# Two gate tiles between the steps of an attention, and mask and maximum in one operation

## The chip, the cores and the metric

The kernel runs on one core of a Trainium2 chip. The metric is the device time of one execution in microseconds. TensorE (PE in the rows) multiplies matrices into PSUM, VectorE (DVE) and ScalarE (ACT) work element by element, GpSimd (POOL) does one kind of subtraction here, and SyncE (SP) issues the loads. Each engine runs its own instructions in their order and waits for the others by semaphores.

## What is computed

Two transformer blocks on 512 tokens of 1024 features, in fp32. The first has four mixers with residuals between them: windowed attention with a sink beside a retention, a memory cross-attention, a gated convolution, and a second memory cross-attention. The second block adds three gated branches (pooling, latent attention, memory attention) and a mixture of 32 experts. The change touches three attentions:

```python
# windowed attention with a sink (8 query heads of 64 features)
scores = jnp.where(valid, einsum(q, k) * d ** -0.5, NEG_INF)
m = jnp.maximum(jnp.max(scores, axis=-1), sink_logit)
p = jnp.exp(scores - m)
denom = jnp.sum(p, axis=-1) + jnp.exp(sink_logit - m)
# latent attention (8 heads), causal
s = jnp.where(k_idx <= q_idx, s * scale, NEG_INF_2);  p = softmax(s)
# memory attention of the second block (4 heads of 128, 256 memory rows), and its gate
y_mem = softmax(q @ k.T * 128 ** -0.5) @ v
merged = gates[:, 0] * (y_pool @ w_br_pool) + gates[:, 1] * (y_mla @ w_br_mla) \
         + gates[:, 2] * (y_mem @ w_br_mem)     # gates = sigmoid(h @ w_gate + b)
```

## The kernel before

Activations lie with features in the 128 partitions and tokens in the columns. A weight matrix is a stream of *units*, 128x1024 blocks, that pass through a ring of three slots: SyncE loads a unit into `w_ring`, ScalarE rounds it into `hi_ring` (`highs_through`, called by `unit_done`), and GpSimd takes the rest into `lo_ring` (`lows`). A slot is loaded again when its low part is done, and rounded again when TensorE has used it. Each product is three products of rounded parts (`three`). `tile` makes one 128x512 output from one unit with 24 of them; `piece` makes a part of a tile, so that a tile can be spread between the steps of something else. Output tiles go round the four PSUM banks `G`; `bank_free` waits until the tile four before has been evacuated.

An attention runs in units `u` (a query tile of 128 tokens, for one or two heads), of which four are in flight: `S` holds the scores of two, two banks of `G` those of the others. For each, TensorE makes scores, VectorE the maximum (`maxima`, into `mx`, and its scaled negative in `nb`), ScalarE the exponentials and their sum (`exps`), VectorE the normalisation (`normalise`), TensorE the transposes (`transposed`), ScalarE the copy out of PSUM (`copy_t`), and TensorE the value products.

In the windowed attention (`swa_max`, 16 units, two heads each, 128 or 256 keys) VectorE first adds the mask to the scores of each head, then reduces, compares with the sink, negates, and makes `snk`, the sink less the maximum. TensorE puts a quarter of a gate tile (`e_ag`, `e_bg`) into each step. In the latent attention (`top`, 32 units, one head each, 128 to 512 keys) the mask covers the last 128 keys. In the second block's memory attention (`scores2`, `one2`, `top2`; 8 units, 4 value products `x2_o`) TensorE has nothing between the steps. Behind it `branch("g_mem", ...)` runs: for every two output tiles two gate tiles from `xa_hi`, and two products with the memory attention's output `yb_hi`, `yb_lo`. The order on all engines is the order in which the program is written. TensorE's product helper is line 1617 and its transposes in the attentions line 1723, so all their rows have these lines.

## Time and profile before

| | us |
|---|---|
| median of three runs | 1772.3 |
| lowest and highest run | 1771.83, 1773.69 |
| the profiled execution | 1771.13 |
| its span | 1769.3 |
| TensorE busy | 1683.5 (95%) |
| VectorE busy | 872.1 (49%) |
| ScalarE busy | 579.2 (33%) |
| GpSimd busy | 541.7 (31%) |

All times in rows count from the start of the span. Products are pipelined: a product's row lasts longer than the distance to the next one, so distances between starts are what adds up. The granted clock is the share of TensorE's full speed of 2.4 GHz; 0.5 is its other level, 1.2 GHz.

### The profile page before, as it was taken

Reading aid. Unit: us, or ns where it says so; the run is one execution under the profiler, and the core shown is the slowest. Engines: PE = TensorE matmul, PEld = TensorE weight load, DVE = VectorE, ACT = ScalarE, POOL = GpSimd, SP = SyncE. Lnnn points to the kernel's source line nnn. Section 1 sums busy time; section 2 is a strip of 40 time slices with the busy share of each in tenths; the row PEclk is TensorE's granted clock in tenths of the full one; section 3 lists DMA queues with packets and bytes.
Section 4 is the critical chain, followed back from the end, with each engine's and each line's share of the span. In section 5 each row is a group of like instructions: output and inputs, shape, how many; then the busy total and the mean of one; then the engine's idle time right before and its main releaser. Section 6 shows DMA issues by size and latency. Waiting matters only on the chain.

```text
span 1769.3 us, 20751 instructions
## 1 busy us (share of the span) xinstructions
PE 1683.5 (95%) x7816; PEld 1260.4 (71%) x7816; DVE 872.1 (49%) x1420; ACT 579.2 (33%) x952; POOL 541.7 (31%) x228
## 2 busy tenths in 40 slices
PE   6999889999999999999998999999989979999996
PEld 4887658887888888887875768888767755556553
DVE  4338576125644466435666754342323554343335
ACT  4116554324322244334424233342333331121112
POOL 3431216731444446732431214464324300000000
PEclk8999999999999999999999999999989989999998
DMA  4221213521232223421220113243213449888871
GB/s 161 95 72 48 72 48 115 172 96 58 92 95 96 95 84 123 163 83 40 93 84 24 60 49 95 96 131 107 84 36 99 165 183 364 323 344 336 340 287 49
DMA packets 50627, 228.08 MB, mean 129 GB/s; under 512 B 6000, under 2 KB 6896, under 8 KB 45936
## 3 DMA queue, kind: packets, MB, share of 16 engines
q1 hardware_dynamic: 48816, 222.08, 35.8%
q10 hardware_dynamic: 1728, 4.87, 0.8%
q8 instruction: 56, 0.92, 0.2%
q14 instruction: 27, 0.22, 0.0%
HBM read 224.82 MB, written 2.10 MB: 128 GB/s over the span
## 4 chain that ended last, share of the span: by engine, by line
PE 90%; DVE 6%; ACT 2%; issue 1%; DMA 0%; ACTq 0%; DVEq 0%; SPq 0%
PE G L1617 72%; PE O L1617 6%; PE S L1617 5%; PE TR L1617 4%; PE TR L1723 1%; DVE mx L973 1%; DVE mx L978 1%; PE G L2156 0%; DVE arena L993 0%; DVE sq L993 0%; ACT arena L545 0%; DVE S L971 0%; DVE U L1608 0%; DVE yb_lo L1004 0%; DMA X<-in_x_in_dram 0%
## 5 line engine op out<-in xcount | busy, mean ns | idle before, releaser
L484 POOL TENSOR_TENSOR lo_ring<-w_ring,hi_ring 128x1024 fp32r<-128x1024 f32 x222 | 541.3, 2439 | 880.8 <-ACT hi_ring L503 880.5
L503 ACT ACTIVATE hi_ring<-w_ring 128x1024 fp32r<-128x1024 f32 x222 | 234.7, 1059 | 687.9 <-PE G L1617 685.7
L1617 PE MATMUL G<-xa_hi,hi_ring 128*128 128x512 f32 x928 | 378.9, 408 | 19.7 <-POOL lo_ring L484 12.3
L1617 PE MATMUL G<-xa_hi,lo_ring 128*128 128x512 f32 x928 | 369.1, 398 | 0.0
L1617 PE MATMUL G<-xa_lo,hi_ring 128*128 128x512 f32 x928 | 369.0, 398 | 0.0
L1617 PEld LDWEIGHTS G<-xa_hi,hi_ring 128*128 128x128 f32 x928 | 176.5, 190 | 64.2 <-issue 14.1
L1617 PEld LDWEIGHTS G<-xa_lo,hi_ring 128*128 128x128 f32 x928 | 176.6, 190 | 42.1 <-issue 1.9
L1617 PEld LDWEIGHTS G<-xa_hi,lo_ring 128*128 128x128 f32 x928 | 176.1, 190 | 42.1
L1617 PE MATMUL G<-yb_hi,hi_ring 128*128 128x512 f32 x388 | 154.1, 397 | 0.0
L1617 PE MATMUL G<-yb_hi,lo_ring 128*128 128x512 f32 x388 | 151.9, 391 | 0.0
L1617 PE MATMUL G<-yb_lo,hi_ring 128*128 128x512 f32 x388 | 151.8, 391 | 0.0
L932 DVE TENSOR_TENSOR arena<-G,RB 128x512 f32<-128x512 f32 x76 | 52.4, 691 | 192.3 <-PE G L1617 191.5
L1617 PEld LDWEIGHTS G<-yb_hi,hi_ring 128*128 128x128 f32 x388 | 73.3, 189 | 16.3 <-issue 1.0
L1617 PEld LDWEIGHTS G<-yb_lo,hi_ring 128*128 128x128 f32 x388 | 73.3, 189 | 16.2 <-issue 1.0
L1617 PEld LDWEIGHTS G<-yb_hi,lo_ring 128*128 128x128 f32 x388 | 73.2, 189 | 15.4
L901 DVE TENSOR_TENSOR sumsq<-sumsq,sq 128x512 f32<-128x512 f32 (+1 forms) x59 | 74.5, 1263 | 2.7 <-ACT sq L516 2.7
L1617 PE MATMUL G<-cm_hi,hi_ring 128*128 128x256 f32 (+1 forms) x224 | 72.1, 322 | 0.0
L1617 PE MATMUL G<-cm_hi,lo_ring 128*128 128x256 f32 (+1 forms) x224 | 70.7, 315 | 0.0
L1617 PE MATMUL G<-cm_lo,hi_ring 128*128 128x256 f32 (+1 forms) x224 | 70.6, 315 | 0.0
L1617 PE MATMUL O<-arena 128*128 128x128 f32 (+2 forms) x224 | 59.8, 404 | 9.3 <-ACT arena L545 5.6
L1532 DVE TENSOR_TENSOR X<-X,S 128x512 f32<-128x512 f32 x64 | 44.0, 688 | 38.5 <-PE S L1617 38.5
L1617 PE MATMUL G<-yb_hi,xa_hi 128*128 128x256 f32 x256 | 60.2, 294 | 2.9 <-DVE yb_hi L1491 2.9
(300 smaller groups left out, 2674.3 us busy)
## 6 DMA issues: line engine op xcount, KB each, us to landing
w_ring<-in_stream_dram SPq DMA_DIRECT2D x222, 512.0 KB, 3.4
arena<-in_w_gu_dram SPq DMA_DIRECT2D x16, 2048.0 KB, 8.1
ex_rings<-in_w_dn_dram SPq DMA_DIRECT2D x40, 512.0 KB, 13.2
ex_low<-in_w_gu_dram SPq DMA_DIRECT2D x8, 2048.0 KB, 12.4
ex_rings<-in_w_gu_dram SPq DMA_DIRECT2D x8, 2048.0 KB, 12.5
arena<-in_w_dn_dram SPq DMA_DIRECT2D x16, 512.0 KB, 11.6
sq<-in_w_dn_dram SPq DMA_DIRECT2D x8, 512.0 KB, 15.1
X<-in_x_in_dram SPq DMA_DIRECT2D x8, 256.0 KB, 5.7
```

Of the source, the lines that this page charges most:

```text
L484: nc.gpsimd.tensor_tensor(lo_ring[:, s, :], w_ring[:, s, :], hi_ring[:, s, :], ALU.subtract).then_inc(low, 1)
L503: nc.scalar.activation(hi_ring[:, m % RING, :], w_ring[:, m % RING, :], ACT.Copy).then_inc(high, 1)
L901: nc.vector.tensor_tensor(sumsq[:, 0:w], sumsq[:, 0:w], sq[:, (base + f) % 2, 0:w], ALU.add).then_inc(ssq, 1)
L932: nc.vector.tensor_tensor(dst, G[:, a % BANKS, 0:w], by, ALU.mult).then_inc(evac, 1)
L973: do(nc.vector.tensor_reduce(mx[:, at(u), 0:heads], s, AX.X, ALU.max))
L978: do(nc.vector.scalar_tensor_tensor(mx[:, at(u), 0:heads], mx[:, at(u), 0:heads], scale, sink, ALU.mult, ALU.max))
L1532: nc.vector.tensor_tensor(X[:, f, :], X[:, f, :], S[:, f % 2, :], ALU.add).then_inc(x_add, 1)
L1617: return nc.tensor.matmul(*args, **kw)
L1723: ins = nc.tensor.transpose(TR[:, b * P:(b + 1) * P], prob(probs, u, b * P, (b + 1) * P), ident[:, :])
```

## The change

Windowed attention: a new `negative_maxima` does, for each head, one operation that adds the mask, multiplies by the negative scale, writes the result over the scores and keeps the minimum of it and of the negated sink, which is `nb`. `snk` is one subtraction from it. The exponential then has scale -1. A vector `nsink` with the negated sinks is made once at the start. Latent attention: `maxima` reduces the columns ahead of the mask, and one operation masks the last 128 and carries the maximum on. Memory attention of the second block: the first two tiles of `g_mem` are cut into eight pieces, one behind the scores of each step; its scores move from banks 2 and 3 to banks 1 and 2, since the first gate tile uses bank 3 and the second bank 0; ScalarE rounds the next weight unit ahead of its last copy.

```diff
+        nsink = sb("nsink", [P, KT])
...
         def score(u, lo, hi):
-            first = ACC0["e_ag"] + u // TT if u < SU["x0"] else 0
+            first = ACC0["e_ag"] + u // TT if u < SU["x0"] else 3 if u >= SU["x2"] else 0
...
-                                             bias=nb[:, at(u), h:h + 1], scale=scale,
+                                             bias=nb[:, at(u), h:h + 1], scale=-1.0 if sink else scale,
...
                 if u + 3 < 8:
                     one2(u + 3)
+                if u == 6:
+                    unit_done("g_mem", 0)
...
+                if mask is None:
+                    do(nc.vector.tensor_reduce(mx[:, at(u), 0:heads], s, AX.X, ALU.max))
                 else:
+                    low = NEG
+                    if mask_at:
+                        do(nc.vector.tensor_reduce(mx[:, at(u), 1:2], score(u, 0, mask_at), AX.X, ALU.max))
+                        low = mx[:, at(u), 1:2]
+                    part = score(u, mask_at, width)
+                    do(nc.vector.tensor_tensor_reduce(part, part, mask, 1.0, low, ALU.add, ALU.max,
+                                                      mx[:, at(u), 0:1]))
...
+            def negative_maxima(u, width, scale, mask, sink):
+                dve.wait_ge(s_full, u + 1)
+                for h in range(2):
+                    part = score(u, h * width, (h + 1) * width)
+                    note(nc.vector.tensor_tensor_reduce(part, part, mask, -scale, nsink[:, sink + h:sink + h + 1],
+                                                        ALU.add, ALU.min, nb[:, at(u), h:h + 1]))
+                settle()
+                nc.vector.tensor_tensor(snk[:, at(u), 0:2], nb[:, at(u), 0:2], nsink[:, sink:sink + 2],
+                                        ALU.subtract).then_inc(s_max, 1)
...
+            sinks = vec[:, VECTORS["sink"][0]:VECTORS["sink"][0] + KT]
+            do(nc.vector.tensor_scalar(nsink[:, :], sinks, -1.0, None, ALU.mult))
...
-            def branch(stage, k0, ready):
+            def branch(stage, k0, ready, begun=0):
                 for f in range(0, KT, 2):
                     a = ACC0[stage] + 2 * f
                     for e in range(2):
-                        tile(stage, f // 2 * 3 + e, xa_hi, xa_lo, acc=a + e)
+                        if f + e >= begun:
+                            tile(stage, f // 2 * 3 + e, xa_hi, xa_lo, acc=a + e)
...
             def scores2(u):
                 hp, t = divmod(u, TT)
-                if u in (0, 2):
-                    pe.wait_ge(evac, ACC0["xq"] + (2 if u == 0 else 4))
+                if u in (0, 2, 3):
+                    pe.wait_ge(evac, ACC0["xq"] + (2, 2, 3, 4)[u])
...
+                e, ks = ((0, (0, 1)), (0, (2, 3)), (0, (4, 5)), (0, (6,)), (0, (7,)), (1, (0, 1, 2)), (1, (3, 4, 5)),
+                         (1, (6, 7)))[u]
+                if u == 5:
+                    pe.wait_ge(o_free, 24 + 2)
+                piece("g_mem", e, xa_hi, xa_lo, ks)
                 if t == TT - 1:
                     pe.wait_ge(pt_ready, base + u + 1)
...
-            pe.wait_ge(o_free, 24 + 2)
-            branch("g_mem", 0, lambda kk: (o_free, 24 + kk + 1))
+            branch("g_mem", 0, lambda kk: (o_free, 24 + kk + 1), begun=2)
```

TensorE, in the second block's memory attention from the first transposes on, before (TR the transposes, S and G from `arena` the scores):

```order
L1723 MATMUL TR<-ident,arena 128x128 [waits prob_t_ready,score_norm]
L1723 MATMUL TR<-ident,arena 128x128 x3
L1617 MATMUL S<-arena 128x256 [waits score_exp]
L1617 MATMUL S<-arena 128x256
L1723 MATMUL TR<-ident,arena 128x128 [waits prob_t_ready,score_norm]
```

And now, G from `xa_hi` and `xa_lo` the gate tile:

```order
L1733 MATMUL TR<-ident,arena 128x128 [waits prob_t_ready,score_norm]
L1733 MATMUL TR<-ident,arena 128x128 x3
L1627 MATMUL S<-arena 128x256 [waits score_exp]
L1627 MATMUL S<-arena 128x256
L1627 MATMUL G<-xa_hi,hi_ring 128x512 [waits acc_evacuated,unit_low]
L1627 MATMUL G<-xa_lo,hi_ring 128x512
L1627 MATMUL G<-xa_hi,lo_ring 128x512
L1627 MATMUL G<-xa_hi,hi_ring 128x512
L1627 MATMUL G<-xa_lo,hi_ring 128x512
L1627 MATMUL G<-xa_hi,lo_ring 128x512
L1733 MATMUL TR<-ident,arena 128x128 [waits prob_t_ready,score_norm]
```

Six products of the first gate tile now stand between the scores and the next transposes.

VectorE, one step of the windowed attention with 256 keys, before:

```order
L971 TENSOR_TENSOR S<-S,RBm 128x256 [waits score_full,dve_order]
L971 TENSOR_TENSOR S<-S,RBm 128x256
L973 TENSOR_REDUCE mx<-S 128x2 [waits dve_order]
L978 SCALAR_TENSOR_TENSOR mx<-mx,vec 128x2 [waits dve_order]
L980 TENSOR_SCALAR nb<-mx 128x2 [waits dve_order]
L981 TENSOR_TENSOR snk<-vec,mx 128x2
```

And now:

```order
L988 ISA S,nb<-S,RBm,nsink 128x256 [waits score_full]
L988 ISA nb 128x1
L988 ISA S,nb<-S,RBm,nsink 128x256
L988 ISA nb 128x1
L991 TENSOR_TENSOR snk<-nb,nsink 128x2 [waits dve_order]
```

Each fused operation is followed by an instruction that writes out its accumulator; the reduction and two small operations are gone, and three waits of VectorE for itself have become one.

## Rows read from the trace of the kernel before

**Rows 1.** The page: the chain that ended last, by engine; rounding of units.

```profile
PE 90%; DVE 6%; ACT 2%; issue 1%; DMA 0%; ACTq 0%; DVEq 0%; SPq 0%
...
L503 ACT ACTIVATE hi_ring<-w_ring 128x1024 fp32r<-128x1024 f32 x222 | 234.7, 1059 | 687.9 <-PE G L1617 685.7
```

**Rows 2.** Busy time by stretch: length, each engine (instructions), granted clock, DMA.

```profile
143.10:200.20 57.10, 52.65 (x313) 44.09 (x313) 48.54 (x148) 38.17 (x102) 9.43 (x4) 1.00 0.15 52
1269.00:1300.40 31.40, 23.56 (x83) 14.77 (x81) 16.36 (x44) 16.30 (x45) 2.34 (x1) 0.78 0.09 30
```

**Rows 3.** TensorE's timeline, windowed attention: start, duration, instruction [idle before it].

```profile
149.45 0.60 PE L1723 MATMUL TR<-ident,sq 128*128 128x128 f32 x4
...
150.57 0.59 PE L1617 MATMUL G<-xa_hi,hi_ring 128*128 128x512 f32 x1
150.99 0.39 PE L1617 MATMUL G<-xa_lo,hi_ring 128*128 128x512 f32 x1
...
153.11 0.60 PE L1723 MATMUL TR<-ident,sq 128*128 128x128 f32 x4
...
157.10 1.16 PE L1617 MATMUL O<-arena 128*128 128x128 f32 x8 [1.15 <-ACT arena L545]
158.10 0.38 PE L1723 MATMUL TR<-ident,arena 128*128 128x128 f32 x2
```

**Rows 4.** Waits, windowed attention: who waited for whom, us, times, longest.

```profile
ACT arena L532 <- DVE snk L981: 10.1, 6, 2.3
...
PE O L1617 <- ACT arena L545: 4.2, 6, 1.2
```

**Rows 5.** VectorE's timeline, windowed attention; then the mask additions' min/median/max.

```profile
148.31 2.06 DVE L978 SCALAR_TENSOR_TENSOR mx<-mx,vec 128x2 f32<-128x2 f32 x1
...
151.54 0.76 DVE L971 TENSOR_TENSOR S<-S,RBm 128x256 f32<-128x256 f32 x2
152.33 0.69 DVE L973 TENSOR_REDUCE mx<-S 128x2 f32<-128x512 f32 x1
...
153.33 0.15 DVE L981 TENSOR_TENSOR snk<-vec,mx 128x2 f32<-128x2 f32 x1
153.45 0.16 DVE L988 TENSOR_TENSOR den<-den,esnk 128x2 f32<-128x2 f32 x1
...
L971 DVE TENSOR_TENSOR G<-G,RBm x16: 422/424/433, 140.2 to 189.5; 128x256 f32<-128x256 f32 x16
L971 DVE TENSOR_TENSOR S<-S,arena x16: 289/294/300, 932.6 to 1028.4; 128x128 f32<-128x128 f32 x16
```

**Rows 6.** TensorE's timeline, memory attention of the second block and gate tiles.

```profile
1275.20 1.11 PE L1723 MATMUL TR<-ident,arena 128*128 128x128 f32 x4 [2.51 <-DVE arena L993]
...
1277.81 0.88 PE L1723 MATMUL TR<-ident,arena 128*128 128x128 f32 x4
...
1282.62 1.97 PE L1617 MATMUL O<-arena 128*128 128x512 f32 x4
1284.43 1.88 PE L1617 MATMUL G<-arena 128*128 128x512 f32 x4
1288.44 0.99 PE L1723 MATMUL TR<-ident,arena 128*128 128x128 f32 x4 [2.13 <-DVE arena L993]
...
1300.40 0.79 PE L1617 MATMUL G<-xa_hi,hi_ring 128*128 128x512 f32 x1
...
1311.94 0.40 PE L1617 MATMUL G<-yb_hi,hi_ring 128*128 128x512 f32 x1
```

**Rows 7.** Busy time by microsecond, columns as in rows 2.

```profile
1275.00:1276.00 1.00, 0.80 (x4) 0.80 (x5) 0.97 (x4) 0.71 (x4) 0.00 (x0) 0.50 0.58 234
...
1278.00:1279.00 1.00, 1.00 (x8) 0.95 (x7) 0.91 (x3) 0.27 (x1) 0.00 (x0) 0.81 0.00 0
```

**Rows 8.** Timeline: TensorE in the latent attention; VectorE behind the memory attention.

```profile
949.57 0.55 PE L1723 MATMUL TR<-ident,sq 128*128 128x128 f32 x3 [0.37 <-DVE sq L993]
...
1301.63 0.69 DVE L1004 TENSOR_TENSOR yb_lo<-O,yb_hi 128x512 fp32r<-128x512 f32 x1 [1.03 <-ACT yb_hi L549]
```

More of the change, by code:

```diff
@@ L963, in rotate_swapped, with maxima @@
                 do(nc.vector.tensor_tensor(dst, sq[:, 0, :], sq[:, 1, :], ALU.add))
-            def maxima(u, heads, width, scale, mask=None, mask_at=0, sink=None):
+            def maxima(u, heads, width, scale, mask=None, mask_at=0):
                 dve.wait_ge(s_full, u + 1)
                 s = score(u, 0, heads * width).rearrange("p (h w) -> p h w", h=heads)
-                if mask is not None:
-                    for h in range(heads):
-                        part = score(u, h * width + mask_at, (h + 1) * width)
-                        note(nc.vector.tensor_tensor(part, part, mask, ALU.add))
-                    settle()
-                do(nc.vector.tensor_reduce(mx[:, at(u), 0:heads], s, AX.X, ALU.max))
-                if sink is None:
-                    nc.vector.tensor_scalar(nb[:, at(u), 0:heads], mx[:, at(u), 0:heads], -scale, None,
-                                            ALU.mult).then_inc(s_max, 1)
-                else:
-                    do(nc.vector.scalar_tensor_tensor(mx[:, at(u), 0:heads], mx[:, at(u), 0:heads], scale, sink,
-                                                      ALU.mult, ALU.max))
-                    note(nc.vector.tensor_scalar(nb[:, at(u), 0:heads], mx[:, at(u), 0:heads], -1.0, None, ALU.mult))
-                    nc.vector.tensor_tensor(snk[:, at(u), 0:heads], sink, mx[:, at(u), 0:heads],
-                                            ALU.subtract).then_inc(s_max, 1)
-                    settle()
@@ new lines, in maxima @@
+                nc.vector.tensor_scalar(nb[:, at(u), 0:heads], mx[:, at(u), 0:heads], -scale, None,
+                                        ALU.mult).then_inc(s_max, 1)
+            def negative_maxima(u, width, scale, mask, sink):
[7 more added lines that the diff above has]
+                                        ALU.subtract).then_inc(s_max, 1)
@@ L1041, in swa_max @@
                 j, t = divmod(u, TT)
-                sink = vec[:, VECTORS["sink"][0] + 2 * j:VECTORS["sink"][0] + 2 * j + 2]
                 w = P if t == 0 else 2 * P
-                maxima(u, 2, w, 64 ** -0.5, swa_m[:, 256 - w:256], 0, sink)
+                negative_maxima(u, w, 64 ** -0.5, swa_m[:, 256 - w:256], 2 * j)
             def swa_low(j):
```

## The prediction

> **What bounds the kernel now.** I read first the chain of work that ended last: 90% of the span is TensorE's, so a change counts only where it shortens TensorE's own sequence [rows 1]. Then the stretches that the diff touches. In the windowed attention (143.1 to 200.2 us) TensorE is busy 52.65 of 57.10 us while VectorE is busy 48.54; in the second memory attention (1269.0 to 1300.4) it is busy 23.56 of 31.40 us, at a mean granted clock of 0.78 [rows 2]. The rest of the kernel runs the same instructions in the same order. Third, what TensorE waits for there. In the windowed attention it is ScalarE's copy of the transposed probabilities, 4.2 us in six waits; and ScalarE is late because its exponentials wait for VectorE's `snk`, 10.1 us in six waits [rows 4]. So VectorE leads that chain from two engines away. In the second memory attention TensorE waits 2.51 us for the first normalisation, 2.13 us for the fifth, and runs part of the time at half clock (1.2 instead of 2.4 GHz) behind both waits [rows 6, 7].
>
> **Part 1: mask and maximum in one operation, windowed attention.** An unhindered step of TensorE lasts 3.66 us (149.45 to 153.11). The next one lasts 4.99 us (to 158.10) with a wait of 1.15 [rows 3], so an idle microsecond in the view stands for 1.33/1.15 = 1.16 us in start times: 4.45 us of idle time [rows 2] are about 5.1 us that could go.
>
> VectorE's maxima of one step now take 1.91 us: 151.54 to 153.45, for two mask additions (0.76 together, 0.38 each), a reduction over 512 columns (0.69) and three small operations [rows 5]. Added are, per step, two fused operations over 256 columns, each with a read of its accumulator as an instruction of its own (the order of the change shows it), and one small subtraction. The trace of before has no such operation. Lower bound: a mask addition with nothing more, 0.38 us. Upper bound: the addition plus half of the 512-column reduction, 0.38 + 0.35 = 0.73 us. I take 0.46 us, since it streams the same operands as the addition: 0.38, and 0.08 for the read, half the 0.15 us of a small operation that nothing holds up. The subtraction takes 0.12 (153.33 to 153.45) and a semaphore trip as much, so a step takes 2 x 0.46 + 0.25 = 1.17 us, 0.74 less than now. All the rest of VectorE's work is 48.54/16 - 1.91 = 1.1 us a step, so it needs 2.3 us against TensorE's 3.66 and leaves the path. What is late next is ScalarE at the fourth step of a head pair, where two table loads and the gate lie between exponentials and copy, and the blocked VectorE: while GpSimd converts weights, one small operation took 2.06 us [rows 5]. That lock stays, but it now falls into slack of 1.4 us a step. I leave 0.5 us for these: **gain 4.6 us**, bounds 0 (at 0.73 us a fused operation, the step is 1.71 us and most of the lead is gone again beside the lock) and 5.8.
>
> Two edits ride along at no cost: the negated sinks at the start (one 128x8 operation before VectorE's first tile, which waits for x to land), and the score banks (3 and 0 become 1 and 2 in the second memory attention). If their cover went, each would cost some 0.2 us.
>
> **Weighing a rule of the Trainium skill.** The rows say that what goes is a long reduction. VectorE: DVE Perf Modes, section Rules for kernel authors, says of chained VectorE operations not to fuse for speed but to lower their number, and here six instructions become five; counted so, a step would save a sixth of 1.91 us, 0.32 us, and the gain would be some 3.9 us instead of 4.6. No row here shows a fused operation.
>
> **Part 2: the same in the latent attention.** There 32 masks cover 128 columns. At the first query tile of a head a reduction goes (0.29 us, the length of the 128-column addition in rows 5) and a read comes: 0.2 us less. At the other three the reduction gets 128 columns shorter (about 0.13 us) and the read costs 0.08: nothing. TensorE waits here for VectorE's normalisation behind the first maximum of a head, 0.37 us in one case [rows 8]. Eight heads, most of them with such a wait: **gain 0.5 us**, bounds -1 (the fused operation a little dearer) and 1.2.
>
> **Part 3: two gate tiles between the attention steps.** The tiles are 48 products, now 1300.40 to 1311.94, 11.54 us behind the attention [rows 6]. Cut into eight pieces they need 11.2 us (0.233 each) and 0.19 us for the first product of each piece behind an fp32 one (150.57 to 150.99 is 0.42) [rows 3]: 12.7 us. Which of it finds idle time?
>
> - Before the second transposes (1277.81) nothing is put in; the wait of 2.51 us ahead of the first ones stays whole [rows 6].
> - From there to the value products at 1282.62 four pieces go in, 21 products: 4.9 + 0.8 = 5.7 us, and 0.3 more, since the clock is half until about 1278.4 [rows 7]. Against that stand some 0.3 us of waits and slow products. TensorE has hardly any gap here, so this is nearly all a delay: the value products start 5.7 us later, at 1288.3.
> - The wait of 2.13 us at 1288.44 [rows 6] stays. VectorE must first take the low parts of two outputs, and ScalarE their high parts, before it normalises the fifth unit, and the piece of this step stands ahead of the value products. The fifth transposes start at 1288.44 + 5.7 = 1294.1.
> - From there TensorE now needs 11.96 us (1288.44 to 1300.40) for four transposes and eight value products, which at full clock would be about 5.6 us (0.5 for each group of transposes, and twice the 1.81 us from 1282.62 to 1284.43): half clock and copies between transposes make the rest. The other 27 products take 6.3 + 0.8 = 7.1 us and cover the waits for the copies. With a stretch of half clock as long as the first one now (1275.0 to 1278.4 [rows 7]), which costs 1.7 us, this becomes 14.4 us: the end is 1308.5.
>
> Now the two tiles are done at 1311.94, then at 1308.5: **gain 3.5 us**. Without a second stretch of half clock it is 5.2 us. With one of 10 us, as now (the mean of 0.78 over 31.4 us means 13.8 us at half clock, 3.4 of them the first [rows 2, 7]), it is 0.2 us. Behind it TensorE goes straight to the branch products, which need the low part of the last output: now it is done at 1302.32, 1.9 us after TensorE has gone on [rows 6, 8], and the nine products of the first three outputs last 2.3 us, so it is hidden by 0.4; without this cover it would cost that 1.9. ScalarE converts the fourth weight unit before the last copy: 1.06 us [rows 1] against a piece of 2.3 us, hidden too. Weight units and their loads move with TensorE. The end of the gate stage and all behind it move as a whole.
>
> **Sum.** 4.6 + 0.5 + 3.5 = 8.6 us. The profiled execution took 1771.13 us (span 1769.3), 1.2 under the median of 1772.3; set against the median this gives **1763.7 us**.
>
> **The rivals.**
>
> 1. *The clock stays low in the interleaved attention.* For it: idle waits stay ahead of both groups, and the second stretch of half clock now lasts 10 us. Against it: that stretch goes with a TensorE that is only partly busy, and the pieces fill it. Part 3 gives 0.2 us: 1767.0 us.
> 2. *The fused operation costs 0.73 us or more.* Then VectorE keeps its lead in the windowed attention and parts 1 and 2 give nothing: 1768.8 us. For it: no row shows the operation. Against it: it reads and writes what the addition does.
> 3. *The fused operation runs at half rate.* From the rows, 128 more columns cost an addition 0.13 us (0.29 to 0.42), so 256 columns at half rate cost 0.27 us more. VectorE's step is 1.7 + 0.9 us, still under 3.66; part 1 loses 0.6, the latent attention 1.4 of at most 32 x 0.13 us: 1765.7 us. DVE: opcode table, instruction layouts, handler registers and perf-mode slots, section Datapath and trigger behaviour, in the Trainium skill says that a result passed back to an earlier stage costs half the rate, and one read by its own stage costs none, which a running minimum needs.
> 4. *Slower.* If the fused operation with its read takes f us, the latent attention pays up to 32 x (f - 0.46), all of it where VectorE leads. From f = 0.7 this eats the gain of parts 3 and 1; at f = 1.0 it is +17 there and +4 in the windowed attention (12 steps of 2.25 instead of 1.91), less 3.5: up to 1790 us, some 1780 at half exposure.
> 5. *Neither part takes hold* (1 and 2 together): 1772.1 us.
>
> **How the numbers follow.** Forecast 0.60, rivals 1 to 5: 0.14, 0.12, 0.06, 0.04, 0.04. All bounds of the sum at their best give 12.2 us, near 1760. The range goes from 1759.5 to 1768.8, which takes in rivals 1 to 3. A difference under 0.2% (3.5 us) can't be told from none: faster 0.88 (forecast, 1, 3 and most of 2), same 0.08, slower 0.04.
>
> **What would show it.** Right: no wait over 0.5 us of the value products for the copy in the windowed attention, which ends some 4.6 us earlier; the fused rows at 0.38 to 0.46 us; transposes of the memory attention spaced by 2.3 to 2.9 us, and the branch products starting at once behind the value products. Wrong: fused rows over 0.7 us; a half clock that lasts over 5 us in the interleaved part; the first branch products waiting for VectorE.

## The result, and the profile after

| | before | after |
|---|---|---|
| median | 1772.07 us | 1759.41 us |
| lowest and highest run | 1770.04, 1773.69 (4 runs) | 1756.99, 1760.42 (4 runs) |
| the profiled execution, its span | 1771.13, 1769.3 us | 1759.42, 1757.5 us |
| ratio, 95% interval | | 0.9927 [0.991, 0.9944] |

The change saves 12.7 us at the median, against 8.6 forecast; the time lies 0.1 us below the forecast range of 1759.5 to 1768.8. In the traces, which differ by 11.8 us of span, it can be told where. The view is TensorE's timeline, and the landmarks are the same instructions in both.

| stretch on TensorE | before | after | difference |
|---|---|---|---|
| start to the first windowed transposes | 143.10 | 144.59 | +1.49 |
| windowed attention | 57.10 | 50.96 | -6.14 |
| from there to the latent attention's first wait of 1.71 us | 737.74 | 738.87 | +1.13 |
| from there to the same wait four heads later | 70.24 | 69.98 | -0.26 |
| from there to the first scores of the memory attention | 260.89 | 261.04 | +0.15 |
| from there to the first product of `w_out` | 101.69 | 93.97 | -7.72 |
| from there to the end | 398.5 | 398.1 | -0.4 |

The first stretch is set by the arrival of the input and of the first weights; in fourteen traces of this study it lasted 141.65 to 144.85 us, without order by kernel, so +1.49 lies within their spread. The third holds about 1 us that the change does cost, see the second traces below. The sixth is the memory attention with its two gate tiles and the rest of the gate stage. It is written as "scores to `w_out`" below.

**Windowed attention.** First its row of busy time by stretch (columns as in [rows 2]), then the one of the memory attention up to the first branch product.

```profile
144.59:195.55 50.96, 50.41 (x314) 44.66 (x312) 37.45 (x127) 38.09 (x99) 9.62 (x4) 1.00 0.17 58
1265.44:1300.21 34.77, 30.12 (x130) 22.26 (x128) 16.42 (x44) 17.27 (x46) 4.74 (x2) 0.95 0.12 40
```

In the first, VectorE is busy 37.45 instead of 48.54 us and TensorE has 0.55 us without work instead of 4.45 [rows 2]. The waits of the same stretch after (who waited for whom, us, times, longest), which answer to [rows 4]:

```profile
ACT arena L533 <- DVE snk L991: 2.4, 2, 1.2
...
PEld O L1627 <- ACT arena L546: 1.2, 2, 1.0
...
PE O L1627 <- ACT arena L546: 0.6, 1, 0.6
```

ScalarE's wait for `snk` (the rows for `arena`) has shrunk from 10.1 to 2.4 us, TensorE's for the copy from 4.2 to 0.6. And one row of before, which I had not used:

```profile
PEld O L1617 <- ACT arena L545: 8.9, 11, 1.6
```

PEld is TensorE's weight load. Before, the weights of the value products came late in 11 steps, not in the six in which TensorE's own row shows idle time. So the step that the prediction called unhindered was hindered a little: it took 3.66 us, with a weight load 0.23 us late in it. The ten full steps last 3.66 to 4.99 us before; after, nine of them last 3.59 or 3.60 us and one 3.55, as in these three rows (TensorE's timeline after):

```profile
147.10 0.60 PE L1733 MATMUL TR<-ident,arena 128*128 128x128 f32 x4
...
150.69 0.60 PE L1733 MATMUL TR<-ident,sq 128*128 128x128 f32 x4
...
154.28 0.60 PE L1733 MATMUL TR<-ident,sq 128*128 128x128 f32 x4
```

The fused operation, on VectorE's timeline after, and below it the latent attention's three forms (min/median/max in ns):

```profile
147.50 2.71 DVE L1002 TENSOR_SCALAR sq<-sq,rcp 128x256 f32<-128x256 f32 x2
150.12 0.48 DVE L988 CUSTOM_DVE_ANT_0 S<-S,RBm,nsink 128x256 f32<-128x256 f32 x1
150.53 0.13 DVE L988 DVE_READ_ACCUMULATOR2_ANT nb<- 128x1 f32 x1
150.53 0.48 DVE L988 CUSTOM_DVE_ANT_0 S<-S,RBm,nsink 128x256 f32<-128x256 f32 x1
150.93 0.14 DVE L988 DVE_READ_ACCUMULATOR2_ANT nb<- 128x1 f32 x1
151.10 0.16 DVE L991 TENSOR_TENSOR snk<-nb,nsink 128x2 f32<-128x2 f32 x1
...
L979 DVE CUSTOM_DVE_ANT_0 G<-G,arena,mx x16: 357/359/360, 931.5 to 1028.8; 128x128 f32<-128x128 f32 x16
L979 DVE CUSTOM_DVE_ANT_0 S<-S,arena x8: 290/296/300, 929.1 to 1022.5; 128x128 f32<-128x128 f32 x8
```

A fused operation over 256 columns has a row of 0.48 us, and the next one starts 0.41 us behind it, at the same time as the read of the first one's accumulator (150.53 twice). The read costs nothing between two of them. A step's maxima take 150.12 to 151.18, 1.06 us. The blocked VectorE of [rows 5] is there too, now 2.71 us in a normalisation, and no wait of TensorE follows it.

**Memory attention.** TensorE's timeline after, which answers to [rows 6]:

```profile
1265.44 1.89 PE L1627 MATMUL S<-arena 128*128 128x256 f32 x8
...
1271.56 0.66 PE L1733 MATMUL TR<-ident,arena 128*128 128x128 f32 x4 [2.51 <-DVE arena L1002]
1272.05 1.03 PE L1627 MATMUL S<-arena 128*128 128x256 f32 x4
1272.73 0.58 PE L1627 MATMUL G<-xa_hi,hi_ring 128*128 128x512 f32 x1
1273.15 0.39 PE L1627 MATMUL G<-xa_lo,hi_ring 128*128 128x512 f32 x1
...
1274.32 0.60 PE L1733 MATMUL TR<-ident,arena 128*128 128x128 f32 x4
...
1281.74 1.88 PE L1627 MATMUL O<-arena 128*128 128x512 f32 x4
...
1287.47 1.11 PE L1733 MATMUL TR<-ident,arena 128*128 128x128 f32 x4 [2.14 <-DVE arena L1002]
...
1300.21 0.79 PE L1627 MATMUL G<-yb_hi,hi_ring 128*128 128x512 f32 x1
```

Both waits stay, as forecast. But the stretch of half clock behind the first one is gone, and the one behind the second has become short. The granted clock is the last figure but two of each row (after, then before):

```profile
1272.00:1275.00 3.00, 3.00 (x18) 2.55 (x17) 2.50 (x10) 1.63 (x7) 0.00 (x0) 1.00 0.04 14
1288.00:1290.00 2.00, 2.00 (x8) 1.56 (x7) 1.55 (x8) 1.38 (x5) 0.00 (x0) 0.50 0.00 0
1291.00:1295.00 4.00, 4.00 (x21) 3.26 (x20) 0.00 (x0) 1.90 (x3) 0.00 (x0) 1.00 0.00 0
```

```profile
1276.00:1278.00 2.00, 2.00 (x7) 1.53 (x6) 0.63 (x3) 1.51 (x5) 0.00 (x0) 0.50 0.03 12
1289.00:1298.00 9.00, 5.98 (x18) 3.36 (x17) 2.32 (x10) 3.30 (x8) 0.00 (x0) 0.50 0.00 0
```

Summed over rows of one microsecond (twice the missing share of the clock), this attention has 13.6 us at half clock before (3.4 and 10.2) and 3.4 after.

### The profile page after: what moved, and what is told of

Its sections match the earlier page's. It is cut to its first block, busy times and chain, and to the rows that moved or that the text cites. A ratio compares the mean times of both kernels' runs of the same rounds, so it can differ in the third digit from the quotient of the medians.

```text
span 1757.5 us, 20745 instructions
## 1 busy us (share of the span) xinstructions
PE 1680.4 (96%) x7816; PEld 1258.8 (72%) x7816; DVE 859.2 (49%) x1429; ACT 579.0 (33%) x952; POOL 542.5 (31%) x228
## 4 chain that ended last, share of the span: by engine, by line
PE 93%; DVE 3%; ACT 1%; issue 1%; DMA 0%; ACTq 0%; DVEq 0%; SPq 0%
PE G L1627 74%; PE O L1627 7%; PE S L1627 6%; PE TR L1627 4%; PE TR L1733 2%; PE G L2171 0%; DVE arena L1002 0%; DVE U L1618 0%; DVE yb_lo L1013 0%; DVE sumsq L1552 0%; DMA X<-in_x_in_dram 0%; ACT xa_hi L519 0%; ACT sq L517 0%; DVE nb L981 0%; DVE arena L1109 0%
## 5 line engine op out<-in xcount | busy, mean ns | idle before, releaser
L1627 PE MATMUL G<-xa_hi,hi_ring 128*128 128x512 f32 x928 | 378.3, 408 | 19.2 <-POOL lo_ring L485 11.8
```

What stands on the lines that cost most here:

```text
L1627: return nc.tensor.matmul(*args, **kw)
```

## The experiments

The questions were: is a fused operation's gain really the shorter path to the maximum; do the parts add up; how much of part 3 is idle time filled and how much is clock; and does the clock follow the program or chance. Time at half clock is always summed as above. Each ratio is against runs of the kernel before taken beside it, whose medians are 1770.3 to 1771.2 us, somewhat under the 1772.1 of the table.

### The fused operations alone

The changed kernel without the pieces, the new score banks and the earlier rounding.

```diff
-                piece("g_mem", e, xa_hi, xa_lo, ks)
...
-            branch("g_mem", 0, lambda kk: (o_free, 24 + kk + 1), begun=2)
+            branch("g_mem", 0, lambda kk: (o_free, 24 + kk + 1))
```

> The kernel before with only the fused mask and maximum, in the windowed and the latent attention; no gate pieces, old score banks. Theory A (the parts are independent and add up): windowed attention 57.1 -> about 51.0 us (-6.1), latent attention -0.8, the second block's memory attention unchanged at about 31.4 us from the first scores to the branch products, and its granted clock again 0.5 from the first wait of 2.5 us on. Time about 1765.2 us, ratio 0.996. Theory B (the clock after the first wait depends on when the attention starts, not on the pieces): the attention starts some 4 to 7 us earlier here, as in the changed kernel, the clock stays at 1.00 behind the first wait, and the memory attention is 1.5 to 2 us shorter without any piece: about 1763.5 us. If the negated sinks at the start cost what the changed kernel's start lost (1.5 us up to the first transposes), the time is 1.5 us higher in either case.

Measured: 1765.77 us, ratio 0.9971 [0.9961, 0.9981], 4.6 to 5.1 us gained. The windowed attention lasts 51.00 us. The clock did not fall behind the first wait of 2.51 us, and fell for 10.2 us behind the second:

```profile
1272.00:1275.00 3.00, 2.82 (x16) 1.91 (x15) 2.77 (x11) 2.81 (x10) 0.00 (x0) 1.00 0.03 12
1285.00:1294.00 9.00, 6.75 (x16) 3.62 (x17) 1.40 (x5) 2.44 (x7) 0.00 (x0) 0.50 0.00 0
```

So the clock behind the first wait stayed up without any piece (against theory A), and scores to `w_out` took 100.38 us instead of 101.69, which is most of the 1.7 us that theory B gives. The time is theory A's.

### The pieces alone

The changed kernel with the masks, reductions and small operations of before in both attentions.

```diff
-                    note(nc.vector.tensor_tensor_reduce(part, part, mask, -scale, nsink[:, sink + h:sink + h + 1],
-                                                        ALU.add, ALU.min, nb[:, at(u), h:h + 1]))
+                    note(nc.vector.tensor_tensor(part, part, mask, ALU.add))
+                settle()
+                do(nc.vector.tensor_reduce(mx[:, at(u), 0:2], s, AX.X, ALU.max))
```

> The changed kernel with the old mask additions and reductions in both attentions: only the eight gate pieces, the score banks and the rounding of the next unit ahead of the last copy. Theory A (the pieces' gain stands by itself): the branch products start 7.6 to 8.1 us earlier against the first scores of the memory attention than before, as in the changed kernel; time about 1764.4 us, ratio 0.9957, and with the fused part alone it adds up to the 12.7 us of both. Theory B (the clock is a matter of when the attention starts): with windowed and latent attention as before, the clock falls to 0.5 behind the first wait of 2.5 us, and the gain is the 3.5 to 5.2 us of the prediction: 1767 to 1768.6 us, with four transposes of the first half spaced by over 2.7 us.

Measured: 1767.92 us, ratio 0.9979 [0.9969, 0.9988]: 3.7 us by the ratio, 2.4 by the medians. The time lies within the 1767 to 1768.6 of theory B, and the clock did fall behind the first wait, as that theory says. Yet scores to `w_out` took 94.43 us, 7.3 less than before, since this time the clock did not fall behind the second wait:

```profile
1281.00:1284.00 3.00, 3.00 (x9) 2.45 (x8) 1.71 (x7) 1.51 (x5) 0.00 (x0) 0.50 0.03 11
1298.00:1306.00 8.00, 7.83 (x42) 6.26 (x43) 2.79 (x11) 4.26 (x9) 1.70 (x1) 1.00 0.00 0
```

Of the 7.3 us a part was lost elsewhere: the trace has 20.4 us at half clock from the retention to the scores instead of 17.0 (1.7 us), and 1.2 us more than before up to the latent attention, outside any such stretch.

### The fused operation in the windowed attention alone

The kernel with the fused operations alone, and in the latent attention the addition over 128 columns and the whole reduction of before.

```diff
-                    do(nc.vector.tensor_tensor_reduce(part, part, mask, 1.0, low, ALU.add, ALU.max,
-                                                      mx[:, at(u), 0:1]))
+                    do(nc.vector.tensor_tensor(part, part, mask, ALU.add))
+                    do(nc.vector.tensor_reduce(mx[:, at(u), 0:heads], s, AX.X, ALU.max))
```

> The kernel before with the fused operation in the windowed attention alone; the latent attention masks and reduces as before, no pieces. Theory A: windowed attention -6.1 us, all else unchanged, about 1766.0 us, so the latent attention's share is the 0.8 us between this and the kernel with both. Rival: the latent attention's fused form is worth nothing or costs (its 128-column operation with its read takes 0.43 to 0.50 us against 0.29 for the addition), and this kernel is as fast as the one with both, within 0.5 us.

Measured: 1769.67 us, ratio 0.9994 [0.9985, 1.0002]. Both expectations missed: the windowed attention lasts 50.97 us, 6.1 less than before, and the kernel is no faster. The trace has 23.8 us at half clock from the retention to the scores, against 17.0 before: a stretch behind the windowed attention that before does not have, and two instead of one behind the latent attention. Rows of the two added ones:

```profile
198.00:201.00 3.00, 3.00 (x9) 2.31 (x8) 0.43 (x1) 0.00 (x0) 0.00 (x0) 0.54 0.53 175
...
1034.00:1040.00 6.00, 5.31 (x12) 3.30 (x12) 0.01 (x1) 1.19 (x2) 0.00 (x0) 0.50 0.00 0
```

6.8 us more at half clock cost 3.4 us, and another 1.1 us are the unexplained ones of the table above; that leaves 1.6 of the 6.1 us, of which the timed runs show 0.7. Between the latent attention's two waits of 1.71 us this kernel takes 70.43 us and the one with both fused operations 69.96, with the same stretches at half clock: 0.5 us for half of the latent attention.

### The changed kernel again

No edit, beside the three kernels that follow.

> The changed kernel, unaltered, beside the three kernels below. Theory A (stretches at half clock come where the clock happens to fall, and differ between executions and programs): ratio to before 0.993 to 0.995, its trace with the same structural steps (windowed attention 51.0 us, 94 us from the first scores of the memory attention to w_out) but not necessarily the same stretches at half clock; e.g. the first wait of 2.5 us may be followed by one. Theory B (the clock is fixed by the program): the trace has half clock in the memory attention only behind the second wait, as in the first trace, and its total at half clock is again within 1 us of 54.6.

Measured: 1759.12 us, ratio 0.9935 [0.9922, 0.9948]. The same program, another pattern: now the clock does fall behind the first wait, as it did before the change, and TensorE's rows there are long:

```profile
1266.56 0.66 PE L1733 MATMUL TR<-ident,arena 128*128 128x128 f32 x4 [2.51 <-DVE arena L1002]
...
1267.73 0.79 PE L1627 MATMUL G<-xa_hi,hi_ring 128*128 128x512 f32 x1
1268.31 0.63 PE L1627 MATMUL G<-xa_lo,hi_ring 128*128 128x512 f32 x1
...
1278.30 1.88 PE L1627 MATMUL O<-arena 128*128 128x512 f32 x4
...
1296.84 0.79 PE L1627 MATMUL G<-yb_hi,hi_ring 128*128 128x512 f32 x1
```

Scores to `w_out` takes 95.62 us with 6.8 us at half clock, 93.97 with 3.4: 1.65 us for 3.4 us, half of it; TensorE is busy throughout both stretches. Theory B, that the program fixes the clock, falls for this kernel. This trace is also the one in which both of the prediction's assumptions on the clock hold.

### Pieces in the first wait

```diff
+            piece("g_mem", 0, xa_hi, xa_lo, (0, 1, 2))
             for u in range(8):
                 transposed(base + u, P2, 4)
...
-                e, ks = ((0, (0, 1)), (0, (2, 3)), (0, (4, 5)), (0, (6,)), (0, (7,)), (1, (0, 1, 2)), (1, (3, 4, 5)),
+                e, ks = ((0, (3,)), (0, (4,)), (0, (5,)), (0, (6,)), (0, (7,)), (1, (0, 1, 2)), (1, (3, 4, 5)),
```

> The changed kernel, but the first piece (nine products, three of the eight feature tiles) stands ahead of the first transposes, and the next four pieces have three products each. The nine products last 2.1 us beside the wait of 2.51 us for the first normalisation. If that wait is idle time of TensorE that a piece can fill, it shrinks to about 0.4 us (0.2 go to the switch between kinds of product) and the distance from the first scores to w_out to 92.0 us from 94.0; time 2 us under the changed kernel. Rival: the wait stays since scores, gate products and transposes share something else; then nothing is gained.

Measured: 1755.66 us, ratio 0.9914 [0.9901, 0.9927], 3.5 us under the changed kernel. The wait shrank to 0.42 us and the half clock is gone from the whole attention, behind the second wait too:

```profile
1271.88 0.66 PE L1733 MATMUL TR<-ident,arena 128*128 128x128 f32 x4 [0.42 <-DVE arena L1002]
...
1285.70 0.66 PE L1733 MATMUL TR<-ident,arena 128*128 128x128 f32 x4 [2.14 <-DVE arena L1002]
```

Scores to `w_out` takes 90.67 us, 3.3 less than after. The clock accounts for 1.7 of it (half of 3.4 us), and the other 1.6 go with a first wait that is 2.1 us shorter. This is one trace; that the full clock behind the second wait comes from filling the first one is not shown, since the pieces alone had it once too.

### Normalisation ahead of the low parts

```diff
-                if u % TT == TT - 1:
+                if u in (TT, 2 * TT - 1):
                     for e in range(2):
-                        j = u // TT * 2 + e
+                        j = (u + 1) // (2 * TT) * 2 + e
                         low_of(x2_o(j), yb_hi[:, j, :], yb_lo[:, j, :], o_free)
```

> The changed kernel, but VectorE takes the low parts of the first two outputs behind the normalisation and maxima of the next unit instead of ahead of them; TensorE's order is unchanged. The prediction said that the wait of 2.13 us before the fifth transposes stays because VectorE must first do the two low parts, and ScalarE their high parts. If so, the wait goes here, and the half clock behind it with it (up to 1.7 us): 92 to 90.3 us from the first scores to w_out, time 2 to 3.8 us under the changed kernel. Rival: ScalarE still makes the two high parts ahead of the next copy, so the wait only moves from the fifth to the sixth transposes: the same time within 0.7 us.

Measured: 1757.43 us, ratio 0.9919 [0.9904, 0.9934], 1.7 us under the changed kernel by the medians. The second wait went, and half of it (1.00 us) came back one step later, which is part of what the rival expected:

```profile
1285.26 0.60 PE L1733 MATMUL TR<-ident,arena 128*128 128x128 f32 x4
...
1287.56 0.66 PE L1733 MATMUL TR<-ident,arena 128*128 128x128 f32 x4 [1.00 <-DVE arena L1002]
```

Scores to `w_out` takes 91.25 us, within the 90.3 to 92 expected, without half clock inside the attention.

### Both, with the pieces where TensorE waits

Nine products ahead of the first transposes, none at the next three, three ahead of the first value products, twelve behind the fifth transposes.

```diff
-                e, ks = ((0, (0, 1)), (0, (2, 3)), (0, (4, 5)), (0, (6,)), (0, (7,)), (1, (0, 1, 2)), (1, (3, 4, 5)),
+                e, ks = ((0, ()), (0, ()), (0, ()), (0, (3,)), (0, (4, 5, 6, 7)), (1, (0, 1, 2)), (1, (3, 4, 5)),
                          (1, (6, 7)))[u]
```

> Both edits, and the pieces put where TensorE waits: nine products ahead of the first transposes, none behind the scores of units 4 to 6, three ahead of the first value products, twelve behind the fifth transposes (beside ScalarE's two high parts), nine, nine and six behind the last three. If the pieces among the first three transposes only delay, and all gaps can be covered: two waits of 2.5 and 2.1 us and one stretch at half clock (1.7 us) go, less 0.2 us, so about 88 to 90 us from the first scores to w_out, and the time is 4 to 6 us under the changed kernel, ratio to before 0.990 or less. Rival: without pieces among the first transposes the copies and normalisations lead there and give back 1 to 2 us.

Measured: 1751.86 us, ratio 0.9894 [0.9879, 0.9908]: 7.3 us under the changed kernel beside it and 19.2 under the one before, the best of this study. Its attention up to the first branch product:

```profile
1264.74:1294.30 29.56, 28.95 (x130) 20.77 (x128) 16.26 (x44) 17.16 (x46) 4.74 (x2) 1.00 0.14 47
```

TensorE has 0.61 us without work, the clock is full throughout in this one trace, and scores to `w_out` takes 88.71 us. The rival's waits among the first transposes are 0.19 us in all.

### Second traces

Before, and the pieces alone, unaltered, one execution each.

> The kernel before, unaltered, for a second trace. In all traces of changed kernels the stretch from the end of the windowed attention to the latent attention's first wait of 1.7 us lasts 738.3 to 739.0 us (an extra stretch at half clock taken off), in the one trace of before 737.7. If that is chance, this trace lies within the others' 738.3 to 739.0; if the changed kernels lose 1.1 us there by their code, it is again 737.7. From the first scores of the memory attention to w_out it is 94.9 us plus half the time at half clock there (101.7 with 13.6 us before).

The second trace of before (1771.72 us) has the same ten stretches at half clock up to 1740 us, and scores to `w_out` 101.53 us. From the windowed to the latent attention it takes 737.5 us, the first one 737.7. The changed kernels, of whatever form, take 738.3 to 739.0, less 1.7 us where they have one more stretch at half clock. So they do lose about 1 us there. Put side by side instruction by instruction, the trace of the fused operations alone falls behind that of before in two places, by 0.5 us each: from 316 to 383 us and from 707 to 770 us (times of before). Between them the shift does not grow, and in the second trace of before it grows at neither. The cause is open. All changed kernels, the pieces alone too, have the new vector `nsink`, and no run leaves it out.

> The kernel with only the pieces again, for a second trace: from the first scores of the memory attention to w_out 92.5 us plus half the time at half clock there (94.4 with 3.4 us in its first trace), so 92.5, 94.2 or 95.9 us. If the stretches at half clock belong to the program they are again one behind the first wait and none behind the second; if not, another pattern.

The second trace of the pieces alone (1766.64 us) takes 93.83 us, with no half clock behind the first wait and 3.4 us behind the second: the reverse of its first trace.

### A reduction put back, ahead of the maximum and behind it

The changed kernel with an unused reduction in each windowed step: over 512 columns ahead of the fused operations; the same behind `snk`; over 256 columns ahead.

```diff
                 dve.wait_ge(s_full, u + 1)
+                do(nc.vector.tensor_reduce(mx[:, at(u), 0:2], RB[:, :].rearrange("p (h w) -> p h w", h=2),
+                                           AX.X, ALU.max))
                 for h in range(2):
```

> The changed kernel with a reduction over 512 columns of RB put ahead of each step's two fused operations in the windowed attention (its result is unused). VectorE's work ahead of the exponentials is then 1.06 + 0.7 = 1.76 us a step, 0.15 less than before the change, and its total 3.0 us a step as before. Theory (the windowed attention gained because VectorE's maximum came sooner): almost all waits come back, 3.5 to 4.5 us of them, and the windowed attention lasts 55.5 to 57 us; time 4.5 to 6 us over the changed kernel. Rival (what counts is the form of the operations, their write into PSUM or the waits of VectorE for itself, not its time): 51 to 52.5 us.

> The same reduction, but behind the step's last operation, after the exponentials are released. VectorE's work per step is the same 3.0 us as in the kernel before and as with the reduction ahead. If it is the time from the scores to the maximum that counts, not VectorE's sum, most of the gain stays: 51 to 53 us. If it is VectorE's sum (a normalisation that comes late behind the reduction), this is as slow as with the reduction ahead, 55.5 to 57 us.

> As the kernel with the reduction ahead of the fused operations, but over 256 columns instead of 512 (about 0.42 us instead of 0.70), its result unused. The windowed attention lasted 50.96 us with nothing ahead (1.06 us from the first fused operation to the subtraction) and 55.15 with 0.7 us more. Theory A (each 0.1 us of the chain costs the same from the start): 0.42/0.70 of the 4.2 us, so 53.5 us. Theory B (TensorE's step hides a chain up to a point, and beyond it the loss is nearly the whole excess of the 12 full steps): at 0.42 us most is still hidden, 51.0 to 52.0 us.

| kernel | VectorE's chain per step | VectorE busy | windowed attention | time |
|---|---|---|---|---|
| after | 1.06 us | 37.45 | 50.96 | 1759.4 |
| 256 columns ahead | 1.5 | 42.54 | 53.01 | 1763.3 (one run) |
| 512 columns ahead | 1.8 | 45.72 | 55.15 | 1766.03, ratio 0.9969 [0.9959, 0.998] |
| 512 columns behind | 1.06 | 46.44 | 52.76 | 1762.95, ratio 0.9955 [0.9938, 0.9971] |
| before | 1.91 | 48.54 | 57.10 | 1772.1 |

The rows of the three (order of the table):

```profile
141.67:194.68 53.01, 51.66 (x313) 44.25 (x312) 42.54 (x144) 37.92 (x99) 9.61 (x4) 1.00 0.17 55
```

```profile
143.02:198.17 55.15, 52.44 (x314) 44.13 (x312) 45.72 (x146) 37.98 (x99) 9.60 (x4) 1.00 0.16 52
```

```profile
143.19:195.95 52.76, 51.52 (x313) 44.53 (x313) 46.44 (x148) 37.93 (x99) 9.51 (x4) 1.00 0.17 56
```

The same 0.7 us a step cost 4.2 us ahead of the maximum and 1.8 behind it, the latter within the 51 to 53 us expected if the way to the maximum is what counts: it counts more than VectorE's sum, but the sum counts too. The 55.15 us lie just below the 55.5 expected. With 256 columns the stretch loses 2.05 us for 0.45 us a step (theory A gave 2.5, theory B 0 to 1), so no lengthening of the chain was free. It is not spread evenly, though: five of the ten full steps keep their 3.59 to 3.61 us, and the other five, most of them the third and fourth of a head pair, last 3.85 to 4.07. In half of the steps TensorE still hides a chain of 1.5 us.

The comparison rests on the stretch alone, not on the times. Behind the first product of `w_out`, which the edits do not touch, their traces last 400.5 to 402.6 us instead of 398.1. In all three VectorE idles 2.2 to 2.4 us ahead of one small instruction near the end, which waits for nothing that the view shows, and TensorE's wait for it lasts 7.3 or 7.4 us instead of 5.1. With 512 columns ahead:

```profile
1751.60 0.06 DVE L1617 MEMSET arena<- 128x1 f32 x1 [2.23 <-issue]
```

## Why the forecast came out as it did

**What bounds the kernel** was read rightly. VectorE led the windowed attention through ScalarE, and shortening its chain gave the gain; putting 0.7 of the 0.85 us back ahead of the maximum took 4.2 of the 6.1 us away.

**Part 1, windowed attention: forecast 4.6, measured 6.1**, above its upper bound of 5.8. Three terms were too small; they overlap, so they do not add up to the miss. The step of 3.66 us taken as unhindered was hindered; without the late weight load it is 3.59 us, which over ten full steps is 0.7 us. The row of the late weight loads would have told it. VectorE's chain became 1.06 instead of 1.17 us: a fused operation takes 0.41, not 0.46, since the read lies beside the next operation, and the 0.25 us for the subtraction and its wait, for the latter half of which the prediction had no row, were right (0.24). At the slope measured with 256 columns (2.05 us of the stretch for 0.45 us a step) the 0.11 us are worth 0.5, an estimate. And 1.16 us of start time for each idle microsecond, taken from one step, was too low: the idle time fell by 3.9 us and the stretch by 6.1. The 0.5 us left for late tables and the lock was about right: one wait of 0.56 us is left. All idle time gone was 5.1 us by the prediction's own sum, and the bound of 5.8 us had no working; neither was a bound.

**The rule of the Trainium skill** (VectorE: DVE Perf Modes, Rules for kernel authors: lower the number of operations, do not fuse for speed) gave 3.9 us. The gain was 6.1, with six instructions become five, so here fusing was worth more than the count says. What went was a pass over 512 columns, 0.69 us.

**Part 2, latent attention: forecast 0.5, measured about 0.4** for its first half, and nothing visible in the second half. Between the two waits of 1.71 us, with the same time at half clock, the five traces without the operation take 70.21 to 70.59 us and eight with it 69.77 to 70.03. The four waits of 0.37 us on which the forecast rests are gone, in both halves (waits for `sq`, before and after):

```profile
PE TR L1723 <- DVE sq L993: 2.6, 6, 0.6
```

```profile
PE TR L1733 <- DVE sq L1002: 1.2, 2, 0.6
```

The 128-column form takes 0.36 us where its start value is a column, against 0.29 for the plain addition, so the forecast's "nothing" for three of four query tiles holds.

**Part 3, memory attention: forecast 3.5, measured 7.7.** That is the step that failed most, in two ways.

- The clock. The sum assumed 3.4 us at half clock behind each wait and took the first one as there before and after. Behind the second it was 3.4, as assumed. Behind the first there was none. In the second trace of the same kernel both stretches are there, and the gain is 6.1 us against before. So 1.65 us of the miss are a draw of the clock, luck in the direction of a larger gain; the forecast could not know it, but could have carried it as a spread.
- The pieces. Even with the assumed clock the value products start 17.87 us behind the first scores (1260.43 to 1278.30) instead of 13.55, a delay of 4.3, not 5.7, and from the fifth transposes to the branch products it is 12.8 us, not 14.4. The sum counted each piece as its products plus 0.19 us for its first one. It also says that nothing is put in ahead of the second transposes; the first piece of six products stands just there, and only the total of 21 products ahead of the value products was right. With the clock full, the traces show what a piece of six costs: transposes to transposes is 2.76 us with it (1271.56 to 1274.32) and 1.53 without, in the kernel with the fused operations alone:

```profile
1271.51 0.65 PE L1731 MATMUL TR<-ident,arena 128*128 128x128 f32 x4 [2.51 <-DVE arena L1000]
1272.01 1.03 PE L1625 MATMUL S<-arena 128*128 128x256 f32 x4
1273.04 0.66 PE L1731 MATMUL TR<-ident,arena 128*128 128x128 f32 x4
```

That is 1.2 us for six products, 0.20 each and nothing for the first. Scores that are followed by transposes hold TensorE 1.03 us (1272.01 to 1273.04); followed by a gate product they hold it 0.68 (1272.05 to 1272.73). The 0.35 us are no idle time in any view, and the piece uses them up: 6 x 0.233 + 0.19 - 0.35 = 1.24 us.

The waits of 2.51 and 2.14 us stayed and the low part of the last output was hidden, as forecast.

**Rival 1** (the clock stays low) had it the wrong way round. In all four traces without pieces the clock fell behind the second wait for 10.2 us. In the eight with pieces in which a wait of 2.13 or 2.14 us is left it fell for 3.4 us six times and not at all twice. This is shown; its worth is only bounded. Before, TensorE was busy for 7.22 of the 10.24 us:

```profile
1288.62:1298.86 10.24, 7.22 (x20) 4.08 (x20) 2.69 (x11) 3.30 (x8) 0.00 (x0) 0.50 0.00 0
```

A full clock could have taken at most half of these 7.22 us away, 3.6 us, and the 3.4 us at half clock after, with TensorE always busy, cost 1.7. So behind the second wait the clock gave at most 1.9 of the 7.7 us, and at most 1.6 more behind the first, where TensorE was busy for 3.2 of 3.4 us. TensorE's idle time within the attention fell by 3.2 us (7.84 to 4.65). The prediction's 0.2 us for this rival took half of the whole 10 us off, waits included, and so made the clock too dear.

**Rivals 2 to 4** needed a dear fused operation; it takes 0.41 us from start to start, 0.03 more than the 0.38 us of the plain additions [rows 5], so no half rate. This agrees with what the Trainium skill (DVE: opcode table, instruction layouts, handler registers and perf-mode slots, Datapath and trigger behaviour) says of an operation in which a stage reads back its own result.

**The sum.** All bounds at their best gave 12.2 us, and 12.7 were measured (11.9 in the later runs beside their own kernel before), since parts 1 and 3 both passed their upper bounds of 5.8 and 5.2 us. Two slips had no weight: rival 3 has 0.9 us a step for the rest of VectorE's work where part 1 has 1.1, and 1311.94 less 1308.5 is 3.4. The parts do not add up in the times: 0.9971 and 0.9979 alone, 0.9927 and 0.9935 together. They do in the stretches that they touch (51.0 us and 92.1 to 92.8 us plus half the time at half clock). What differs is the clock elsewhere. Each stall of the kernel (behind the retention, in the latent attention, before `w_out`) can be followed by a stretch at half clock, and one of 3.4 us more or less is 1.7 us of time. The forecast's "moves as a whole" leaves this out. What decides it is open: before showed the same pattern twice, the changed kernel and the pieces alone two patterns each.

## What to carry to other kernels

- When an engine waits now and then, look at its weight loads' waits too, and compare its steps with the fastest step of the program, not with the first that shows no bracket. Shortening the chain ahead of the wait then gains more than the idle time.
- Work that can be moved freely belongs into the waits: the same 48 products gave 7.7 us spread evenly between the steps and, with VectorE's order changed too, 13.0 us in the waits (88.71 instead of 101.69), since there they fill idle time, and in the one trace of that kernel the clock stayed up.
- A gain of a few microseconds in one stage has to be read in that stage. One more stretch at half clock elsewhere, which the edit does not touch, hides 1.7 us of it, as in the kernel that gained 6.1 us in its stage and nothing in its time.

## What was not expected of the hardware

The stretches at half clock lasted 3.4, 6.8, 10.2 or 13.7 us in every trace, wherever they stood, but for the one at the kernel's end (17.5 to 20.4 us). The wait of 2.5 us ahead of the first transposes, behind the same products, was followed by one in 5 of 12 traces; twice the same program once had it and once not. And TensorE's fp32 scores hold it 0.35 us longer when fp32 transposes follow than when a rounded product does (1.03 and 0.68 us from start to start). An unused reduction in the windowed attention went with an idle VectorE of 2.2 to 2.4 us, some 1550 us behind its end, in three kernels of three; nothing in the views explains it.
